# A ninth gate/up block by seven products, and the second norm's factor spread in the middle of a weight tile

## The reference, cut to what matters

```
x = x + mix @ w_out                       # this sum is x1 in the kernel
h2 = rms_norm(x, g_ffn)                   # x * rsqrt(mean(x*x) + 1e-6) * g_ffn
x = x + (silu(h2 @ w_ffn_gate) * (h2 @ w_ffn_up)) @ w_ffn_down
```

## Time and profile before

| what | us |
|---|---|
| median of 3 runs | 857.26 (856.96 to 857.64) |
| the profiled execution, its own time | 857.08 |
| its span, first to last instruction | 855.3 |
| plain gate/up blocks, first matmul to first of the seven products | 502.2 to 569.4 |
| seven-product blocks | 569.4 to 732.0 |
| down projection and output | 732.0 to 855.3 |

### The profile page before, as it was taken

How to read it: one execution, slowest core, us unless ns; L and a number is a source line. 1 busy time by engine, 2 the same in 40 slices (tenths; PEclk the granted TensorE clock), 3 DMA queues, 4 the chain that set the end, 5 groups by cost and what they waited for, 6 DMA issues and landing times.

```text
span 855.3 us, 15076 instructions
## 1 busy us (share of the span) xinstructions
PE 848.7 (99%) x5171; PEld 729.5 (85%) x5171; DVE 571.8 (67%) x790; ACT 361.2 (42%) x575; POOL 250.2 (29%) x266
## 2 busy tenths in 40 slices
PE   9999999999999999999999999999999999999998
PEld 8888788888887888888877888889999999888886
DVE  6458976567934564545587666889999999533334
ACT  6312353313345665756333343444545544222221
POOL 0689995010020000001220220056666664000000
PEclk9999999999999999999999999999999999999999
DMA  8439237634465543512635232332334333322212
GB/s 312 148 107 238 75 123 147 216 121 137 132 220 161 172 139 107 169 50 78 179 118 197 78 105 89 100 88 85 113 109 115 105 98 114 103 93 92 92 70 98
DMA packets 103494, 108.87 MB, mean 127 GB/s; under 512 B 11712, under 2 KB 69296, under 8 KB 103328
## 3 DMA queue, kind: packets, MB, share of 16 engines
q1 hardware_dynamic: 96544, 94.25, 35.4%
q10 hardware_dynamic: 5504, 10.52, 3.8%
q0 software_dynamic: 1408, 3.61, 1.9%
HBM read 94.38 MB, written 13.96 MB: 127 GB/s over the span
## 4 chain that ended last, share of the span: by engine, by line
PE 93%; DVE 4%; issue 1%; POOL 1%; ACT 0%; DMA 0%; SPq 0%; ACTq 0%; POOLq 0%
PE ps L1555 46%; PE ps L1870 18%; PE ps L1890 13%; PE ps L1832 6%; PE ps L1750 2%; PE ps L1779 1%; PE ps L1721 1%; PE ps L1735 1%; DVE early L1075 1%; PE ps L1725 1%; PE ps L1591 1%; PE ps L1602 1%; DVE late L1537 1%; DVE w_lo L1427 1%; DVE h_lo L1423 1%
## 5 line engine op out<-in xcount | busy, mean ns | idle before, releaser
L660 DVE TENSOR_TENSOR w_lo<-w_raw,w_hi 128x1024 fp32r<-128x1024 f32 x109 | 139.3, 1278 | 204.7 <-ACT w_hi L654 204.7
L654 ACT ACTIVATE w_hi<-w_raw 128x1024 fp32r<-128x1024 f32 x109 | 115.3, 1058 | 282.1 <-PE ps L1555 160.3
L1555 PE MATMUL ps<-w_hi,hT_hi 128*128 128x512 f32 x280 | 109.6, 392 | 0.7 <-DVE early L993 0.7
L1555 PE MATMUL ps<-w_hi,hT_lo 128*128 128x512 f32 x280 | 109.0, 389 | 0.0
L1555 PE MATMUL ps<-w_lo,hT_hi 128*128 128x512 f32 x280 | 109.0, 389 | 0.0
L1555 PE MATMUL ps<-hT_hi,w_hi 128*128 128x512 f32 x224 | 91.8, 410 | 0.0
L1555 PE MATMUL ps<-hT_hi,w_lo 128*128 128x512 f32 x224 | 87.7, 392 | 0.0
L1555 PE MATMUL ps<-hT_lo,w_hi 128*128 128x512 f32 x224 | 87.4, 390 | 0.0
L498 POOL TENSOR_TENSOR early<-early 128x16 f32<-128x16 f32 (+5 forms) x125 | 76.0, 608 | 9.7
L1870 PE MATMUL ps<-h_hi,w_hi 128*128 128x256 f32 x256 | 72.8, 285 | 0.6 <-DVE w_lo L1427 0.5
L1870 PE MATMUL ps<-h_lo,w_hi 128*128 128x256 f32 x256 | 72.4, 283 | 0.0
(11 more groups left out here) (249 smaller groups left out, 1793.0 us busy)
## 6 DMA issues: line engine op xcount, KB each, us to landing
w_raw<-in_w_in SPq DMA_DIRECT2D x108, 256.0 KB, 3.7
w_raw<-in_w_ffn_down SPq DMA_DIRECT2D x44, 256.0 KB, 2.8
w_raw<-in_w_ffn_gate SPq DMA_DIRECT2D x64, 128.0 KB, 2.2
w_raw<-in_w_ffn_up SPq DMA_DIRECT2D x64, 128.0 KB, 2.4
z_d<-early ACTq DMA_DIRECT2D x7, 1024.0 KB, 5.0
late<-z_d SPq DMA_DIRECT2D x96, 64.0 KB
w_raw<-in_w_out SPq DMA_DIRECT2D x16, 256.0 KB, 3.0
late<-z_d SPq DMA_DIRECT2D x12, 256.0 KB
```

What stands on the lines that cost most here:

```text
L654: nc.scalar.activation(w_hi[:, j % WSPL], w_raw[:, j % WRAW], ACT.Copy).then_inc(w_hi_done, 1)
L660: nc.vector.tensor_tensor(w_lo[:, j % WSPL], w_raw[:, j % WRAW], w_hi[:, j % WSPL].bitcast(F32), ALU.subtract).then_inc(w_lo_done, 1)
L1555: ins = T.matmul(ps[:, bank0 + m], lhsT, rhs, start=first and h == 0 and k == 0, stop=last and h == 1 and k == 2)
```

## The change

`FP` becomes 2: two plain blocks and nine by seven products. The factor is spread after two of the four columns of block 0's tile 2. DVE makes the normed activations at once after the copy, on both sides of the low part of the next tile, and only then empties block 0's sums; differences, partners and the low parts of block 1 follow in a new order. ACT's list is the same work less four roundings and a pair of silus. PE's loop over the plain blocks 1 and 2 becomes straight code for block 1. SP's program is the same but for its counts.

```diff
-FP = 3
+FP = 2
...
             silus(0, 2)
-            for j in range(1, 5):
+            for j in range(1, 4):
                 hi(W_FFN + j + 4, j)
-                if j >= 3:
-                    partner_hi(j - 3)
-            for m in range(2):
-                act.wait_ge(ffn_evac, 4 + m + 1)
-                nc.scalar.activation(sg[:, m], sg[:, m], ACT.Silu).then_inc(silu_done, 1)
-            for j in range(1, 4):
-                hi(W_FFN + j + 8, j)
                 if j < 3:
-                    partner_hi(j + 1)
+                    partner_hi(j - 1)
+            for i in (2, 3):
+                partner_hi(i)
...
             V.tensor_copy(norm_all[:, :], ps[:, 5]).then_inc(norm2_eps, 1)
-            lo(W_FFN + 4, 4)
             dve.wait_ge(norm2_eps, 2)
-            swiglu(0)
...
+            for k in range(4):
+                normed(k)
+            lo(W_FFN + 4, 4)
+            for k in range(4, KT):
+                normed(k)
+            columns_out(0)
             lo(W_FFN + 5, 1)
-            for k in range(KT):
-                normed(k)
-            lo(W_FFN + 6, 2)
+            gated(0)
             for n in range(3):
                 difference(n)
+            partner_lo(0)
+            lo(W_FFN + 6, 2)
+            difference(3)
+            partner_lo(1)
             lo(W_FFN + 7, 3)
-            difference(3)
-            partner_lo(0)
-            lo(W_FFN + 8, 4)
-            partner_lo(1)
-            swiglu(1)
-            for j in range(1, 4):
-                lo(W_FFN + j + 8, j)
-                if j < 3:
-                    partner_lo(j + 1)
+            for i in (2, 3):
+                partner_lo(i)
             for i in range(3):
                 op_lo(FP, 0, i)
             partner_lo(4)
...
-            ffn(0, 2)
+            ffn(0, 2, (0, 1))
             pe.wait_ge(norm2_done, 1)
...
             ins.then_inc(norm2_spread, 1)
+            ffn(0, 2, (2, 3))
             ffn(0, 3)
-            with pe.Fori(1, FP) as f:
+            for f in range(1, FP):
                 for j in range(4):
                     ffn(f, j)
```

More of the change, by code:

```diff
@@ L956, in _ @@
             for m in range(2):
-                act.wait_ge(ffn_evac, 8 + m + 1)
+                act.wait_ge(ffn_evac, 4 * FP - 4 + m + 1)
                 nc.scalar.activation(sg[:, m], sg[:, m], ACT.Silu).then_inc(silu_done, 1)
@@ L1817, in _, with ffn @@
                             split_rows(mix_lo_done, 0), 4 * c))
-            def ffn(f, j):
+            def ffn(f, j, columns=range(4)):
                 w = W_FFN + j + 4 * f
                 pe.wait_ge(w_lo_done, w + 1)
-                for m in range(4):
+                for m in columns:
                     if j == 0:
-                        if isinstance(f, int):
+                        if f == 0:
                             pe.wait_ge(dve_evac, DE_MIX + m + 1)
@@ L1826, in ffn @@
                             pe.wait_ge(ffn_evac, 4 * f - 3 + m)
-                    if isinstance(f, int) and m == 0:
+                    if f == 0 and m == 0:
                         pe.wait_ge(h2_lo_done, 2 * j + 2)
```

## The result

The changed kernel takes 860.08 us in the median (858.93 to 861.65, 7 runs), the kernel before 857.40 (856.96 to 858.05, 7 runs). The ratio is 1.0030, with a 95% interval of 1.0018 to 1.0042: slower, by 1.5 to 3.6 us. Forecast were 859.1 and a range of 857.0 to 860.4.

What follows compares the result with a forecast made beforehand. PE was taken to bound the kernel, except a 25 us stretch off PE before product 6. One more steady block, 20.16 us, less product 6's 18.3 us earlier start gives +1.86: median 859.1 us, range 857.0 to 860.4.

Steps and rivals of the forecast that it cites:

- a second delay: Rival, block 1: low parts of tiles 6 and 7 late, PE stands there too; 1 to 1.5 us more, 860.3; chance 0.08.
- product 6: First seven-product block: PE's product 6 starts at 560.4, 18.3 us earlier than before, after a 3.6 us wait.
- the copy of the factor: Block 0, tile 2, on DVE: starts at 517.84 instead of 520.58, a 2.7 us head start.
- first matmul of block 1: PE at block 1: waits for block 0's column 0, starts near 526.3; 0.55 us charged with the restart.
- low part of tile 6: DVE, block 1's tile 2: runs from 535.7 to 536.9, just in time for PE at 537.3; the load behind is late.
- POOL's first sum: POOL, before the seven products: starts at 541.0, 5.24 us behind the start of tile 6's low part.
- first product: PE, start of the first seven-product block: at 548.16, after block 1's 21.76 us.
- POOL against DVE: DVE up to partner 4: sums and DVE instructions alternate, costing DVE about 1.1 us at each of four sums; operand 2 ends 548.8.
- The straight code in place of the loop: PE's blocks 1 and 2: no price in the trace, taken as 0, bounded from above by 0.8 us.
- The block count wins: Rival: DVE's list fits, only the 1.60 us gain remains; 855.7, or 856.2 with block 1 delayed; chance 0.10.
- Partly hidden: Rival: POOL and DVE block each other less, or a sum slips in earlier; 857.3 to 858.5, no change; chance 0.22.
- The quicker block: Rival: the extra seven-product block takes an estimated 18.3 us instead of 20.16; 857.3; chance 0.02.

Runs made afterwards that it cites:

- e5: e3 with DVE also waiting for POOL's first sum before the low part of block 1's tile 3; 859.76 us, ratio 1.0031 to the kernel before.
- e8: Changed kernel with DVE waiting for POOL's first sum between partner 2 and partner 3; 859.91 us, ratio 1.0029 to the kernel before.
- e1: Changed kernel with sixteen unused 256-token matmuls added on PE between products 5 and 6 of the first seven-product block; 859.28 us, ratio 1.0024 to the kernel before.
- e6: e5 with the factor spread after one column of tile 2 and all eight normed activations before tile 4's low part; 859.30 us, ratio 1.0021.
- e11: Changed kernel with e3's order, spread after one column, POOL's second sums from operand 2, block 1's sums emptied between operands; 856.59 us, ratio 0.9987.
- e4: Changed kernel without the four activation differences, leaving out 5.0 us of DVE work; 858.77 us, ratio 1.0019 to the kernel before.
- e3: Changed kernel with the low part of block 1's tile 2 moved ahead of the third difference and partner 0; 859.39 us, ratio 1.0024.
- e7: Changed kernel with the factor spread after all of tile 2, as in the kernel before; 862.41 us, ratio 1.0063 to the kernel before.
- e9: Changed kernel with POOL's sums for the first seven-product block's second half allowed after operand 2, not 4; 857.55 us, ratio 1.0001.

## Why the prediction was right

*Direction and size.* Slower by 1.86 us was forecast, 2.7 measured (1.5 to 3.6). The interval holds the forecast. Part of this is luck: 860.08 lies just above the 858.3 to 859.9 that the prediction gave to its forecast, and inside the whole range only by the room that was left for a second delay. That delay did not come; the fall of the clock, which was not in the sum, took its place. The trace has 1.86 + 0.44 for product 6 + 0.75 for the clock = 3.05.

*The steps,* forecast against trace less 0.20: the copy of the factor 517.8, 517.9; first matmul of block 1 at 526.3, 526.4; low part of tile 6 at 535.7, 535.8; POOL's first sum 541.0, 541.2; first product 548.2, 548.3; product 6 at 560.4, 560.8; the idle time before it over 2 us, 2.20; later blocks 20.16, 20.16. The way of working that did this was to lay the new list of DVE on the old rows, instruction by instruction, with the distance between starts rather than the durations.

*Off by 0.4 us: how POOL and DVE alternate.* The step "POOL against DVE" let each sum in behind the DVE instruction that was running. The first sum stood through two more, and operand 2 ended at 549.3 in place of 548.8. From partner 4's start on the distance to product 6 is as forecast (11.60 against 11.64). The end of that stretch moved by no more, because what counts is the sum of both (e5, e8). On PE it shows as a wait of 0.9 us in place of 0.4 before product 3.

*Missing, 0.75 us: the clock.* The prediction charged the 3.6 us of waits (3.9 in the trace) once. The last of them is followed by PE at 1.2 GHz; no row of the kernel before has such a stretch, but the waits themselves were forecast, and I did not ask what they would set off. e1 prices it at 0.7.

*The straight code in place of the loop* cost nothing: block 1 takes 21.86 us, and its 0.1 over 21.76 is the restart behind the wait; in e6 and e11, without that wait, it is 21.76.

*The rivals.* "The block count wins" needed 2.9 us from DVE; e4 shows that in this order even 5 us less work ahead of tile 7 does not give it. The reason which I gave against it (a full list from 518.6 on) was therefore only half the reason: the part behind tile 7 binds by itself. "Partly hidden" took the exclusion of POOL and DVE for soft; in every stretch looked at it is hard (e5's 1.5 us won behind tile 7 came back ahead of it), except beside PSUM reads. "A second delay" did not come: the low parts of tiles 6 and 7 were in time. The quicker block did not come either; the steady spacing of 256-token matmuls is 0.120 us after as before, against the 0.109 estimated by the rule of the Trainium skill (TensorE: Matmul & The Clock Gate, Back-to-back issue gap).

## What to carry to other kernels

Where two engines exclude each other, add their work up as one engine's and look for what can run beside instructions that don't take part; reordering the rest moved idle time about here and won 0.25 us at most (e3, e5, e8). A stage that is short of PE work by a block also has a block less to hide its preparation in: compare the preparation's length behind the last event that PE gates with what PE does meanwhile, before counting matmuls saved. And when a change adds a wait of a few microseconds on PE, look at the clock column behind it.

## What the runs showed of the hardware that was not expected

**The clock falls behind a wait of 2.2 us.** In the changed kernel's trace PE waits in the first seven-product block 0.9 us before product 3, 0.5 before product 5 and 2.4 before product 6, counted as the distance between starts less 0.12 (the row gives 2.20 for the last); 1.4 us after product 6 starts, the granted clock goes to 0.50, and matmuls come every 0.213 us until 565.7. Of its seven executions five have a mean clock of 0.998 and take 859.96 to 861.65 us, two have 1.000 and take 858.93 and 859.22. The traces of e3, e4, e5 and e8 have the same wait before product 6 and the same fall; e6 and e7 have the wait and 1.00 in their traces. Of the 60 executions of these seven kernels 27 have a mean clock of 0.998 or less. e1, which leaves 0.3 us of the wait, e9, where the longest wait is 0.8 us, and e11, where it is 1.1, show no fall in this stage, and none of their 33 executions is below 0.999. So the wait allows the fall and doesn't always bring it. This spreads the changed kernel's times more than those of the kernel before. The Trainium skill (TensorE: Matmul & The Clock Gate, Part 1: The HAM clock gate (the "warmup" mystery)) knows two levels, 1.2 and 2.4 GHz, and the rows agree.

**Exclusion of DVE and POOL is not always alternation.** A POOL sum that meets DVE instructions with two SBUF inputs usually gets in behind the one that runs (2.2 to 2.3 us in place of 1.3). The first sum in the changed kernel, in e1, e3, e7 and e9 stood for 3.2 to 5.2 us, until DVE had nothing ready. In e11, with the same order on both engines at that place as e3 and the sum again starting 0.04 us behind the low part of tile 7, it lasted 2.33. What decides stays open; no run was made for it.
